# Second down projection of a Hymba-style block: 14 of its k groups computed in units of Strassen's scheme

## The reference

```python
h = h + 0.5 * swiglu(rms_norm(h, ffn2_norm[l]), ffn2_w_gate[l], ffn2_w_up[l], ffn2_w_down[l])
return rms_norm(h, final_norm)
# swiglu(x, w_gate, w_up, w_down) = (jax.nn.silu(x @ w_gate) * (x @ w_up)) @ w_down
```

## Time and profile before

| | |
|---|---|
| median of 3 runs | 1881.05 us (1881.0 to 1881.74) |
| span of the profiled execution, the only time the page gives for it | 1881.5 us |
| TensorE busy | 1863.3 us, 99% |
| VectorE busy | 1076.0 us, 57% |
| ScalarE busy | 880.4 us, 47% |
| second down projection in that execution | about 1634.7 to 1874.2 us |
| matmuls in it | 1056 |
| TensorE's mean granted clock | 0.999 |

### The profile page before, as it was taken

How to read it: one execution, slowest core, us unless ns; L and a number is a source line. 1 busy time by engine, 2 the same in 40 slices (tenths; PEclk the granted TensorE clock), 3 DMA queues, 4 the chain that set the end, 5 groups by cost and what they waited for, 6 DMA issues and landing times.

```text
span 1881.5 us, 28825 instructions
## 1 busy us (share of the span) xinstructions
PE 1863.3 (99%) x10881; PEld 1582.7 (84%) x10881; DVE 1076.0 (57%) x1161; ACT 880.4 (47%) x1072; POOL 11.0 (1%) x23
## 2 busy tenths in 40 slices
PE   8999999999999999999999999999999999999998
PEld 7888888888888888999998888888888888888886
DVE  5555555555554545688867856555555555455444
ACT  7444444444444444754534655444444444444443
POOL 1000000000000000000000000000000000000000
PEclk9999999999999999999999999999999999999999
DMA  7777667777667667565433557777677766676664
GB/s 247 216 216 218 212 208 218 231 225 218 215 182 228 217 214 222 182 187 147 136 114 103 187 176 251 237 218 216 213 215 217 213 212 211 204 234 196 194 191 144
DMA packets 207848, 380.34 MB, mean 202 GB/s; under 512 B 16016, under 2 KB 35728, under 8 KB 207504
## 3 DMA queue, kind: packets, MB, share of 16 engines
q1 hardware_dynamic: 206912, 378.46, 65.3%
q10 hardware_dynamic: 336, 0.60, 0.1%
q0 software_dynamic: 512, 0.06, 0.0%
HBM read 360.19 MB, written 18.87 MB: 201 GB/s over the span
## 4 chain that ended last, share of the span: by engine, by line
PE 95%; DVE 2%; ACT 1%; DMA 1%; issue 1%; SPq 0%; ACTq 0%; DVEq 0%
PE psB L343 40%; PE psA L343 40%; PE psB L869 5%; PE psA L869 4%; PE psM L343 1%; DVE wlo L326 1%; PE psA L880 1%; PE psB L534 1%; DMA raw<-in_w_in 1%; DVE y L1093 0%; DMA x<-in_x 0%; PE psM L1937 0%; DVE score L1185 0%; DVE top L1184 0%; PE psT L1270 0%
## 5 line engine op out<-in xcount | busy, mean ns | idle before, releaser
L326 DVE TENSOR_TENSOR wlo<-raw,whi 128x1024 fp32r<-128x1024 f32 (+1 forms) x648 | 787.6, 1217 | 752.3 <-ACT whi L317 742.7
L317 ACT CAST whi<-raw 128x1024 fp32r<-128x1024 f32 (+1 forms) x648 | 676.5, 1046 | 921.7 <-PE psB L343 383.6
L343 PE MATMUL psA<-whi,xh 128*128 128x512 f32 (+1 forms) x736 | 283.9, 386 | 0.0
L343 PE MATMUL psA<-wlo,xh 128*128 128x512 f32 (+1 forms) x736 | 283.4, 385 | 0.0
L343 PE MATMUL psA<-whi,xl 128*128 128x512 f32 (+1 forms) x736 | 283.3, 385 | 0.0
L343 PE MATMUL psB<-whi,xh 128*128 128x512 f32 x704 | 274.0, 389 | 0.0
L343 PE MATMUL psB<-whi,xl 128*128 128x512 f32 x704 | 273.9, 389 | 0.0
L343 PE MATMUL psB<-wlo,xh 128*128 128x512 f32 x704 | 273.9, 389 | 0.0
L343 PEld LDWEIGHTS psA<-whi,xh 128*128 128x128 f32 x736 | 138.4, 188 | 27.6
L343 PEld LDWEIGHTS psA<-whi,xl 128*128 128x128 f32 x736 | 138.4, 188 | 27.5
L343 PEld LDWEIGHTS psA<-wlo,xh 128*128 128x128 f32 x736 | 138.4, 188 | 27.4
(11 more groups left out here) (387 smaller groups left out, 2120.3 us busy)
## 6 DMA issues: line engine op xcount, KB each, us to landing
raw<-in_ffn_w_gate SPq DMA_DIRECT2D x176, 512.0 KB, 4.1
raw<-in_ffn_w_up SPq DMA_DIRECT2D x176, 512.0 KB, 4.5
raw<-in_ffn_w_down SPq DMA_DIRECT2D x176, 512.0 KB, 4.2
raw<-in_w_in SPq DMA_DIRECT2D x80, 512.0 KB, 3.7
raw<-in_w_out SPq DMA_DIRECT2D x32, 512.0 KB, 4.1
quads_dram<-stage SPq DMA_DIRECT2D x88, 128.0 KB, 2.3
stage<-quads_dram SPq DMA_DIRECT2D x22, 512.0 KB, 6.5
x<-in_x SPq DMA_DIRECT2D x4, 512.0 KB, 7.4
```

What stands on the lines that cost most here:

```text
L317: nc.scalar.copy(whi[:, slot, :, 0:ncol], raw[:, slot, :, 0:ncol]).then_inc(hi_ready, 1)
L326: nc.vector.tensor_tensor(wlo[:, slot, :, 0:ncol], raw[:, slot, :, 0:ncol], whi[:, slot, :, 0:ncol].bitcast(F32), ALU.subtract).then_inc(l ...
L343: mm = nc.tensor.matmul(ps[:, tb, 0:ncol], lhs[:, k0 + t, tok], rhs[:, slot, t, 0:ncol], start=(first and t == 0 and p == 0), stop=(last a ...
```

## The change

In the second down projection (f = 1) the blocks of columns are taken in pairs (even and odd, m = 0 and 1). In each pair some k groups, 6 in the first and 8 in the second, are computed as units: the two token blocks and the two column blocks of the pair form a 2x2 scheme for each k group, whose two k tiles are the inner index, and seven products take the place of eight. A unit uses two weight groups, the one of the even and the one of the odd columns.

Four products use the weights as they are or sums of activations alone (`unit_products`); they go into psT, psA, psM and psB. Three use sums of weights as well (`sum_products`) and come behind the next plain group. `down_order` writes the list: first `LEAD` plain groups, then the units with the inner plain groups spread between them, then `TAIL` plain groups. VectorE makes the sums of weights in `unit_sums` (four additions of 128x512, one of them in place in `raw`), behind which stand both `split_lo` of the unit. The sums are split by a copy on ScalarE (`unit_hi`) and a subtraction on VectorE (`unit_lo`); `col_lo` is the same memory as `col_sum`. The sums of activations for four k tiles at a time are made in `block_sums` (eight operations of 128x256) and split in `block_sums_hi` and `block_sums_lo`; they lie in `xl` and `xh`. The results of the products are added to `x` in the eight steps of `close_pair`, two behind each of four groups from the fifth after the last unit of a pair. Of the seven block products of a unit, those into psA and psB also collect the plain groups.

SP's loads follow the same list, written out instead of a loop over the second half. The squares of f = 3 go into `stage` instead of psT. The Bacc call gets `dynamic_dma_scratch_size=4096`. The first down projection has no units, and its list is that of before.

```diff
+UNITS = ((0, 0), (6, 8))
+LEAD = ((0, 0), (11, 5))
+TAIL = ((0, 0), (6, 11))
...
+def down_order(f, m):
+    units, lead, tail = UNITS[f][m], LEAD[f][m], TAIL[f][m]
+    plain = [("plain", part, j) for part in range(2) for j in range(units, GF)]
+    if not units:
+        return plain
+    inner = plain[lead:len(plain) - tail]
+    items = plain[:lead]
+    for i in range(units):
+        items.append(("unit", None, i))
+        if i < units - 1:
+            items += inner[i * len(inner) // (units - 1):(i + 1) * len(inner) // (units - 1)]
+    return items + plain[len(plain) - tail:]
...
+        act_sum = at("act_sum", [P, 4, SU, P], xl)
+        act_lo = at("act_lo", [P, 4, SU, P], xl, dt=F32R)
+        act_hi = at("act_hi", [P, 4, SU, P], xh, dt=F32R)
+        col_sum = sb("col_sum", [P, 3, COLS])
+        col_lo = at("col_lo", [P, 3, COLS], col_sum, dt=F32R)
+        col_hi = sb("col_hi", [P, 3, COLS], F32R)
...
+        Q1, Q5, Q6, Q7 = psT[:, 0:COLS], psT[:, COLS:], psM[:, 0:COLS], psM[:, COLS:]
...
+        def unit_products(down, unit, j, g, first, last):
+            gate, up = (down + g) % SLOTS, (down + g + 1) % SLOTS
+            def product(into, h, l, w, v, start, stop):
+                for p, (lhs, rhs) in enumerate(((h, w), (h, v), (l, w))):
+                    mm = nc.tensor.matmul(into, lhs, rhs, start=(start and p == 0), stop=(stop and p == 2))
+                return mm
+            def tokens(t, tb):
+                return [arr[:, KT * j + t, tb * P:tb * P + P] for arr in (hh, hl)]
+            def sums(k):
+                return [arr[:, k, j, :] for arr in (act_hi, act_lo)]
+            def columns(slot, t):
+                return [arr[:, slot, t, :] for arr in (whi, wlo)]
+            def column_sums(k):
+                return [arr[:, k, :] for arr in (col_hi, col_lo)]
+            wait_group(down, 0, 0, g)
+            product(Q1, *tokens(0, 0), *columns(gate, 0), first, last)
+            product(psA[:, 0, :], *tokens(1, 0), *columns(gate, 1), False, last).then_inc(group_used, 1)
+            wait_group(down, 0, 0, g + 1)
+            if j % 2 == 0:
+                nc.tensor.wait_ge(act_lo_ready, j // 2 + 1)
+            product(Q7, *sums(2), *columns(up, 0), first, last)
+            product(psB[:, 0, :], *sums(3), *columns(up, 1), first, False).then_inc(group_used, 1)
+            def sum_products():
+                nc.tensor.wait_ge(col_lo_ready, unit + 1)
+                product(Q6, *sums(1), *column_sums(1), first, last)
+                product(Q5, *sums(0), *column_sums(0), first, last)
+                product(psA[:, 1, :], *tokens(1, 1), *column_sums(2), False, last).then_inc(unit_used, 1)
+            return sum_products
...
+            for i, (m, kind, part, j, g) in enumerate(down_items(f)):
+                split_hi(down, 0, 0, g)
+                if kind == "unit":
+                    nc.scalar.wait_ge(col_step, 4 * unit + 2)
+                    split_hi(down, 0, 0, g + 1)
+                    unit += 1
+                elif i and down_items(f)[i - 1][1] == "unit":
+                    unit_hi(unit - 1)
+                if i == GD + SLOTS:
                     turned_hi(FC - 1)
-                if j > GF and j % GF == 2 * SLOTS - 1:
...
+                if f == 1 and i in (5, 7, 9, begin + 7):
+                    block_sums_hi((5, 7, 9, begin + 7).index(i))
+                if f == 1 and i in (begin + 5, begin + 8):
+                    squares_act(3, (begin + 5, begin + 8).index(i))
+            if f == 1:
+                squares_act(3, 2)
+        def unit_hi(unit):
+            nc.scalar.wait_ge(col_step, 4 * unit + 4)
+            if unit:
+                nc.scalar.wait_ge(unit_used, unit)
+            nc.scalar.copy(col_hi[:, :, :], col_sum[:, :, :]).then_inc(col_hi_ready, 1)
+        def block_sums_hi(b):
+            nc.scalar.wait_ge(act_step, 8 * b + 8)
+            nc.scalar.copy(act_hi[:, :, 2 * b:2 * b + 2, :], act_sum[:, :, 2 * b:2 * b + 2, :]).then_inc(act_hi_ready, 1)
+        def unit_sums(down, unit, g):
+            gate, up = (down + g) % SLOTS, (down + g + 1) % SLOTS
+            wait_raw(nc.vector, down + g)
+            wait_raw(nc.vector, down + g + 1)
+            if unit:
+                nc.vector.wait_ge(unit_used, unit)
+            tt(col_sum[:, 0, :], raw[:, gate, 0, :], raw[:, up, 0, :], ALU.add).then_inc(col_step, 1)
+            nc.vector.wait_ge(col_step, 4 * unit + 1)
+            tt(raw[:, up, 0, :], raw[:, up, 0, :], raw[:, up, 1, :], ALU.add).then_inc(col_step, 1)
+            tt(col_sum[:, 1, :], col_sum[:, 0, :], raw[:, up, 1, :], ALU.add).then_inc(col_step, 1)
+            nc.vector.wait_ge(col_step, 4 * unit + 3)
+            tt(col_sum[:, 2, :], col_sum[:, 1, :], raw[:, gate, 1, :], ALU.add).then_inc(col_step, 1)
+        def unit_lo(unit):
+            nc.vector.wait_ge(col_hi_ready, unit + 1)
+            tt(col_lo[:, :, :], col_sum[:, :, :], col_hi[:, :, :].bitcast(F32), ALU.subtract).then_inc(col_lo_ready, 1)
+        def block_sums(b):
+            def whole(into, t, tb):
+                where = (slice(None), slice(4 * b + t, 4 * b + 4, 2), slice(tb * P, tb * P + P))
+                tt(act_sum[:, into, 2 * b:2 * b + 2, :], hh[where].bitcast(F32), hl[where].bitcast(F32), ALU.add)\
+                    .then_inc(act_step, 1)
...
+        def block_sums_lo(b):
+            nc.vector.wait_ge(act_hi_ready, b + 1)
+            two = slice(2 * b, 2 * b + 2)
+            tt(act_lo[:, :, two, :], act_sum[:, :, two, :], act_hi[:, :, two, :].bitcast(F32), ALU.subtract)\
+                .then_inc(act_lo_ready, 1)
...
...
+            for i, (m, kind, part, j, g) in enumerate(down_items(f)):
+                if kind == "unit":
+                    unit_sums(down, unit, g)
+                    split_lo(down, 0, 0, g)
+                    split_lo(down, 0, 0, g + 1)
+                    unit += 1
+                else:
+                    split_lo(down, 0, 0, g)
+                    if i and down_items(f)[i - 1][1] == "unit":
+                        unit_lo(unit - 1)
+                if i == SLOTS - 1:
+                    gate_up(FC - 1)
+                    turn_quads(FC - 1)
+                if i == GD + SLOTS + 1:
+                    turned_lo(FC - 1)
...
+                if i in (4, 6, 8, begin + 6):
+                    block_sums((4, 6, 8, begin + 6).index(i))
+                if i in (6, 8, 10, begin + 8):
+                    block_sums_lo((6, 8, 10, begin + 8).index(i))
+                for k in range(2):
+                    past = i - last_unit[k] - 5
+                    if 0 <= past < 4:
+                        close_pair(k, 2 * past)
+                        close_pair(k, 2 * past + 1)
+                if i == begin + 3:
+                    add_down(f, down, 1)
+                if i in (begin + 9, begin + 12):
+                    gain_dve((begin + 9, begin + 12).index(i))
+            if f == 1:
+                gain_dve(2)
...
+            for m in range(2):
+                begun, left = set(), None
+                for m_, kind, part, j, g in down_items(f):
+                    if m_ != m:
+                        continue
+                    if kind == "unit":
+                        if j == 0 and m == 0:
+                            nc.tensor.wait_ge(act_ready, (f + 1) * FC)
+                        if j == 0 and m == 1:
+                            nc.tensor.wait_ge(closed, 7)
+                            nc.tensor.wait_ge(x_added, before_down + 2)
+                        left = unit_products(down, unit, j, g, j == 0, j == UNITS[f][m] - 1)
+                        begun.add("odd half")
+                        unit += 1
+                        continue
...
+                    if part not in begun and m == 1:
+                        if f == 1 and part == 0:
+                            nc.tensor.wait_ge(closed, 1)
+                        else:
+                            nc.tensor.wait_ge(x_added, before_down + part + 1)
+                    if (m, part, j) == (0, 0, (KF - 4) // KT):
                         nc.tensor.wait_ge(hl_ready, (f + 1) * FC)
-                    if f == 1 and c == DC - 1 and j >= GF - SLOTS:
+                    if f == 1 and g >= DC * GF - SLOTS:
                         continue
-                    project_tokens((psA, psB)[c % 2], hh, hl, down, 0, 0, c * GF + j, j * KT,
-                                   j == 0, j == GF - 1)
+                    project_tokens((psA, psB)[part], hh, hl, down, 0, 0, g, j * KT,
+                                   part not in begun, j == GF - 1 and not (f == 1 and part == 0),
+                                   open_half=0 if part == 1 and "odd half" in begun else None)
+                    begun.add(part)
+                    if left:
+                        left()
+                        left = None
...
```

More of the change, by code:

```diff
@@ L64, with down_items @@
 CONST_WIDTH = 2816
+def down_order(f, m):
[10 more added lines that the diff above has]
```

(81 more changed lines are left out.)

44 lines of the change are left out of this document (37 added, 7 removed).

## The result

The changed kernel takes 1896.8 us (median of 4 runs, 1895.5 to 1898.0) against 1881.4 us before: ratio 1.0083, 95% interval 1.0071 to 1.0095, so 15.4 us slower. The forecast was 1889.3 us with a range up to 1896: the sign and most of the working held, nearly half of the loss was missing, and the time lies 0.8 us above the range.

The account below looks back on a forecast made before the run. TensorE, busy 99% of the span, was taken as the bound: -9.5 (matmuls) + 7.4 (five short waits) + 8.4 (two long waits) + 2.0 (lead-in) = +8.3 us, on the median 1881.05 giving 1889.3 us; range 1885 to 1896.

Parts of the forecast that it names:

- What bounds the kernel, the matmuls removed: Second down projection: TensorE's matmuls and waits alone count; 42 matmuls fewer at 0.2267 us, -9.5 us.
- The chain behind `unit_used`: From the sum products' end to the next unit's first matmul: 4.20 us; second pair waits five times 1.48, twice 4.20.
- the 13 to 22: The prediction is wrong if TensorE's waits in the stage sum to under 13 us or over 22.
- VectorE's work: Second down projection: some 97 us more on VectorE, 214 of some 240 us; fits on average, so order decides.
- The lead-in: Block sums and splits on VectorE ahead of the first unit make TensorE late: 2.0 us taken, bounds 0 and 4.
- The edits at nothing: `close_pair`, last block sum, SP's loads written out, `squares_act` into `stage`, waits on `closed`, smaller scratch: no cost.
- rival 2: Matmuls behind the two long waits run at 1.2 GHz, 3.2 us each: 1895.7 us, or 1892.5 with one; chance 0.15.
- the chain's bounds: Chain of additions and split ahead of a unit: 3.6 to 4.8 us; over seven waits -4.2 or +4.2.

Follow-up runs that it names:

- the list with two everywhere: Changed kernel with LEAD of the second pair 4 instead of 5 and TAIL 10 instead of 11, two plain groups between any two units: 1886.95 us.
- a better order within the chain: Changed kernel with the `split_lo` for a unit's first weight group ahead of the four additions on VectorE: 1884.75 us.
- the one with the sums spread: Changed kernel with the second and third sums of activations moved later, between the units of the first pair: 1894.38 us.

## Why the prediction was wrong, step by step

- **What bounds the kernel, the matmuls removed:** right. 42 fewer, -9.5 us, and no loss outside the stage is seen: against the trace of the smaller scratch alone the span is 14.3 us longer (1893.7 against 1879.4) and the stage 14.6.
- **The chain behind `unit_used`:** right, to 0.04 us. 4.20 forecast, 4.24 measured where TensorE has nothing in hand, and 1.49 for 1.48 where it has one plain group. That its parts were off against each other is luck: VectorE starts 0.53 behind the last matmul's start and not 0.43, the additions take 2.66 (1772.69 to 1775.35) and not 2.61, and TensorE follows the end of `wlo` (1775.35 + 1.22) after 0.05 and not 0.17. All waits together, 18.5 us, lie in the 13 to 22 that the prediction named. The units with three plain groups between them don't wait. That the buffer is the cause, and not the work, is shown by the second buffer (17 us less with the same work), and the dependence on the plain groups by the list with two everywhere.
- **VectorE's work:** too high, without effect on the sum. 97 us more were forecast for the stage, its busy time rose by 83.4 (117.0 to 200.4). By my estimate most of the difference is the overlap of 0.09 between neighbours, which busy time counts once, over 120 more operations.
- **The lead-in:** 2.5 for 2.0; the working from the earlier trace rows gave 2.5, and I took off for an earlier landing. Group 6 didn't land earlier: its cast starts 12.7 us into the stage (1644.96 - 1632.26) and started at 12.5 before.
- **The edits at nothing:** right. The closing of the pairs and the smaller scratch are not seen in the time.
- **The step that failed: the sum took the clock as unchanged.** It stood as rival 2 with a chance of 0.15 and decided against the forecast: both long waits in the trace of after, and in the repeat, are followed by matmuls 0.43 apart at a granted clock of 0.50. The row that spoke for it was the only one of a long idle time, and I let the absence of a long wait in mid-kernel count against it, where it only said nothing. The price that I gave it was too high: 6.4 us from the length of the slow stretch at the kernel's start, 3.2 measured, as 7 spacings of 0.43 follow each wait and not 16. The Trainium skill (TensorE: Matmul & The Clock Gate, section Why this matters for your kernels) has the rule that an idle stretch between bursts of matmuls puts the clock back to half. The traces agree for the waits of 4.24 us, after which the clock was 0.50.
- **A term not in the sum:** 2.4 us. The matmul behind a wait comes 0.10 late (ten waits, 1.1 us), and the nine matmuls of the sum products, some behind them and some behind a wait stand up to 0.238 apart instead of 0.2267 (1.3 us). That the shape was the same I had taken for the price being the same. What spaces them is open; no run here takes it apart.
- **The range:** with 1.1 + 1.3 + 3.2 the sum is 8.3 + 0.5 + 5.6 = 14.4. My range took in the chain's bounds and rival 2 at one end, but not both kinds of loss together.

## What to carry to other kernels

When an engine that is always busy gets work that another must prepare, ask from which event the preparation may start, and what the busy engine has in hand from that event on; the other engine's idle share did not tell it here. A single buffer between "used" and "make the next" turned a hidden chain into a wait at seven uses here; a second buffer took 17.3 us off the stage, a better order within the chain 11.9. A wait of TensorE of some 4 us is to be priced with the matmuls behind it at half the clock, here 1.6 us each time.

## What the runs showed of the hardware that I had not expected

- Waits of 4.24 us were followed by 6 to 10 spacings of 0.43 us in all six cases (two each in the traces of the changed kernel, its repeat and the one with the sums spread). Of two equal waits of 2.85 us one had this effect and one had not, and none of the waits of 1.49 us in five traces had it.
- The slow matmuls need not start with the first behind the wait: behind the wait of 2.85 us six came at the full pace first.
- A chain of waits and operations over three engines repeated to 0.01 us: the short waits of the second pair are 1.71 to 1.72 us between matmul starts in every trace that has them.
- The first matmul behind a wait takes 0.31 to 0.34 us to the next one at a granted clock of 1.00, those behind it 0.23 to 0.24.
